# Expert stage of a two-block transformer kernel: every piece of the down weights split in full, the low part of the features on GpSimd

## The reference

```python
def hier_moe(h, wg, bg, we, be, w_gate, w_up, w_down):
    ...
    ids = (g_sel * EXPERTS_PER_GROUP + top_i).reshape(-1).astype(jnp.int32)
    order = jnp.argsort(ids)
    tok = order // TOP_K
    xs = xf[tok]
    hg = lax.ragged_dot(xs, w_gate.astype(xs.dtype), sizes)
    hu = lax.ragged_dot(xs, w_up.astype(xs.dtype), sizes)
    ys = lax.ragged_dot(jax.nn.silu(hg) * hu, w_down.astype(xs.dtype), sizes)
    ys = ys * gates.reshape(-1)[order][:, None].astype(ys.dtype)
    y = jax.ops.segment_sum(ys, tok, num_segments=t)
```

## Time and profile before

| | |
|---|---|
| median of 3 runs | 1083.66 us (1079.57 to 1084.92) |
| the profiled execution | 1080.93 us, its span 1079.1 us |
| PE (matmul) busy | 1034.6 us, 96% of the span |
| DVE busy | 842.9 us, 78% |
| ACT busy | 665.2 us, 62% |
| POOL busy | 33.0 us, 3% |
| first and last transposes of the hidden values in a full unit | start 622.28 and 1035.19 us |

### The profile page before, as it was taken

How to read it: one execution, slowest core, us unless ns; L and a number is a source line. 1 busy time by engine, 2 the same in 40 slices (tenths; PEclk the granted TensorE clock), 3 DMA queues, 4 the chain that set the end, 5 groups by cost and what they waited for, 6 DMA issues and landing times. The chain is left out here.

```text
span 1079.1 us, 14950 instructions
## 1 busy us (share of the span) xinstructions
PE 1034.6 (96%) x5574; PEld 872.7 (81%) x5574; DVE 842.9 (78%) x1091; ACT 665.2 (62%) x832; POOL 33.0 (3%) x40
## 2 busy tenths in 40 slices
PE   7999999999998899989889999999999999999996
PEld 6777999999998777889778787878787777878775
DVE  5855766766777556677757889999999899999977
ACT  5554655555555645556333677777777777777764
POOL 1001000000000100100020000000000000000000
PEclk9999999999999999999999999999999999999999
DMA  9634545646424443233311789989998998999881
GB/s 349 244 117 137 194 169 184 196 157 234 156 91 150 158 144 130 81 118 118 117 32 34 285 327 368 371 348 390 349 388 351 374 363 352 378 359 386 339 318 43
DMA packets 82711, 253.61 MB, mean 235 GB/s; under 512 B 4160, under 2 KB 42176, under 8 KB 62656
## 3 DMA queue, kind: packets, MB, share of 16 engines
q1 hardware_dynamic: 82624, 252.50, 62.2%
HBM read 251.44 MB, written 1.05 MB: 234 GB/s over the span
## 5 line engine op out<-in xcount | busy, mean ns | idle before, releaser
L1021 DVE TENSOR_TENSOR WL<-raw,WH 128x2048 fp32r<-128x2048 f32 x232 | 497.5, 2175 | 110.0 <-ACT WH L543 109.7
L543 ACT ACTIVATE WH<-raw 128x2048 fp32r<-128x2048 f32 x232 | 421.5, 1823 | 91.2 <-PE bank L1910 74.9
L1908 PE MATMUL bank<-WH,MXH 128*128 128x512 f32 x552 | 219.4, 397 | 1.6 <-DVE CV L1316 0.9
L1910 PE MATMUL bank<-WH,MXL 128*128 128x512 f32 x552 | 216.0, 391 | 0.0
L1909 PE MATMUL bank<-WL,MXH 128*128 128x512 f32 x552 | 215.5, 390 | 0.0
L1908 PE MATMUL bank<-HTH,WH 128*128 128x256 f32 x576 | 166.1, 288 | 6.2 <-DVE CV L1316 2.6
L1910 PE MATMUL bank<-HTH,WL 128*128 128x256 f32 x576 | 163.6, 284 | 0.0
L1909 PE MATMUL bank<-HTL,WH 128*128 128x256 f32 x576 | 163.6, 284 | 0.0
L1908 PE MATMUL bank<-WH,HTH 128*128 128x512 f32 x348 | 139.7, 401 | 7.2 <-DVE HTL L1044 2.4
L1909 PE MATMUL bank<-WL,HTH 128*128 128x512 f32 x348 | 137.1, 394 | 0.0
L1908 PEld LDWEIGHTS bank<-WH,MXH 128*128 128x128 f32 x552 | 104.4, 189 | 23.2 <-issue 2.3
(11 more groups left out here) (393 smaller groups left out, 1098.6 us busy)
## 6 DMA issues: line engine op xcount, KB each, us to landing
raw<-in_exp_w_up SPq DMA_DIRECT2D x52, 1024.0 KB, 7.6
raw<-in_exp_w_gate SPq DMA_DIRECT2D x52, 1024.0 KB, 8.1
raw<-in_exp_w_down SPq DMA_DIRECT2D x52, 1024.0 KB, 6.7
raw<-in_w_in SPq DMA_DIRECT2D x34, 1024.0 KB, 5.1
raw<-in_w_up SPq DMA_DIRECT2D x22, 1024.0 KB, 5.4
raw<-in_w_down SPq DMA_DIRECT2D x11, 1024.0 KB, 5.2
raw<-in_w_out SPq DMA_DIRECT2D x8, 1024.0 KB, 5.0
raw<-in_w_o SPq DMA_DIRECT2D x4, 1024.0 KB, 5.6
```

What stands on the lines that cost most here:

```text
L543: e.activation(WH[i % HL][:, 0:n], raw[i % RAW][:, 0:n], ACT.Copy).then_inc(a_wh, 1)
L1021: e.tensor_tensor(l, r, h.bitcast(F32), ALU.subtract).then_inc(v_wl, 1)
L1908: e.matmul(out_, ah, bh, start=start, stop=False)
L1910: return e.matmul(out_, al, bh, start=False, stop=stop)
```

## The change

Of the down weights every piece is split in full, and the hidden values with them (512 columns instead of 384), so the native products and the plain copy in `TMP` are gone; `is_mixed` goes, and SP's loads wait for the low part alone. GpSimd gets a unit loop of its own and makes the features' low part for the units from 2 on (two tensor_tensors of 128x512 from `XST` and the high part, each after its own copy on ScalarE). On ScalarE the copy of d1 moves from the end of a unit to the next unit (or the last one), behind that unit's features and norm column.

```diff
-def is_mixed(i):
-
-    return i >= unit_base(1) and (i - unit_base(1)) % 6 == 5
...
-        hidden = HTH[:, 0:6, :].rearrange("p a b -> p (a b)").rearrange("p (i k c) -> p i k c", i=4, k=3)
+        hidden = HTH[:, :, :].rearrange("p a b -> p (a b)").rearrange("p (i k c) -> p i k c", i=4, k=4)
...
+        def features_low(u, tile, k):
+
+            xs4, ks = XST[k].rearrange("p k (t c) -> p k t c", t=NT), slice(4 * k, 4 * k + 4)
+            return (XCL[u % 2][:, ks, :].unsqueeze(2), xs4[:, :, bass.ds(tile, 1), :],
+                    XCH[u % 2][:, ks, :].bitcast(F32).unsqueeze(2))
...
-                    e.wait_ge(*((p_used, j + 1) if is_mixed(j) or is_native(j) else (v_wl, split_count(j))))
+                    e.wait_ge(*((p_used, j + 1) if is_native(j) else (v_wl, split_count(j))))
...
-                n = PC // 2 if is_mixed(i) else PC
-                e.activation(WH[i % HL][:, 0:n], raw[i % RAW][:, 0:n], ACT.Copy).then_inc(a_wh, 1)
+                e.activation(WH[i % HL][:, :], raw[i % RAW][:, :], ACT.Copy).then_inc(a_wh, 1)
...
-                e.activation(HIH[u % 2], bank[TBK][:, 0:384].rearrange("p (k c) -> p k c", k=3),
-                             ACT.Copy)
-                e.activation(TMP[:, u % 2, 0:128], bank[TBK][:, 384:512], ACT.Copy).then_inc(a_tmpc, 1)
+                e.activation(HIH[u % 2], bank[TBK][:, :].rearrange("p (k c) -> p k c", k=4),
+                             ACT.Copy).then_inc(a_hih, 1)
 
             def unit(u):
...
                 if u > 1:
+                    split(i - 1)
                     split(i)
                     split(i + 1)
...
                 split(i + 4)
-                split(i + 5)
 
             def last_unit(u):
                 i = unit_base(u + 1)
+                split(i - 1)
                 split(i)
                 turn_hidden(u)
...
-                n = PC // 2 if is_mixed(i) else PC
-                r, h, l = raw[i % RAW][:, 0:n], WH[i % HL][:, 0:n], WL[i % HL][:, 0:n]
-                e.tensor_tensor(l, r, h.bitcast(F32), ALU.subtract).then_inc(v_wl, 1)
+                e.tensor_tensor(WL[i % HL][:, :], raw[i % RAW][:, :], WH[i % HL][:, :].bitcast(F32),
+                                ALU.subtract).then_inc(v_wl, 1)
...
-                e.wait_ge(a_tmpc, u + 1)
+                e.wait_ge(a_hih, u + 1)
                 if u > 1:
                     e.wait_ge(p_used, unit_base(u))
-                e.tensor_tensor(HIL[u % 2], bank[TBK][:, 0:384].rearrange("p (k c) -> p k c", k=3),
+                e.tensor_tensor(HIL[u % 2], bank[TBK][:, :].rearrange("p (k c) -> p k c", k=4),
                                 HIH[u % 2].bitcast(F32), ALU.subtract).then_inc(v_hil, 1)
...
                 if u > 1:
                     load_tile(u)
                     load_code(u)
-                    features_low(u)
                     e.wait_ge(v_hid, u - 1)
...
+            def unit(u):
+                tile = e.value_load(TBI[u:u + 1, 1:2], min_val=0, max_val=NT - 1)
+                if u == 2:
+                    e.wait_ge(s_xcl, 2)
+                for k in range(2):
+                    e.wait_ge(a_xch, 2 * u + 1 + k)
+                    m = e.tensor_tensor(*features_low(u, tile, k), ALU.subtract)
+                m.then_inc(s_xcl, 1)
+
+            def more(u):
+                with e.If(count > u):
+                    unit(u)
+                    if u + 1 < UNITS:
+                        more(u + 1)
+
+            for u in range(2, LEAST):
+                unit(u)
+            more(LEAST)
             row_powers("out")
...
-                for k in range(3):
+                for k in range(4):
...
                         m = three(bank[banks[hf]][:, :], HIH[u % 2][:, k, :], HIL[u % 2][:, k, :], wh[:, k % 2, hs],
-                                  wl[:, k % 2, hs], k == 0, False)
-                    if k == 1:
+                                  wl[:, k % 2, hs], k == 0, k == 3)
+                    if k % 2:
                         m.then_inc(p_used, 1)
-                w = raw[(i + 1) % RAW][:, PC // 2:PC]
-                for hf in range(2):
-                    m = e.matmul(bank[banks[hf]][:, :], TMP[:, u % 2, 0:128], w[:, hf * 512:(hf + 1) * 512], start=False,
-                                 stop=True)
-                m.then_inc(p_used, 1)
```

More of the change, by code:

```diff
@@ L429, in build @@
                                                      "sege", "vv", "og", "gsq", "emx", "stc", "ogt", "nexp", "csq", "cum"))
-        a_xth, a_route, a_xst, a_selT, a_xch, a_sg, a_tmpc, a_yh, a_selL, a_fo = (
-            sem("a_" + n) for n in ("xth", "route", "xst", "selT", "xch", "sg", "tmpc", "yh", "selL", "fo"))
+        a_xth, a_route, a_xst, a_selT, a_xch, a_sg, a_hih, a_yh, a_selL, a_fo = (
+            sem("a_" + n) for n in ("xth", "route", "xst", "selT", "xch", "sg", "hih", "yh", "selL", "fo"))
         v_wl, v_ms, v_h0, v_coll, v_ang, v_ropm, v_rope, v_lam, v_nm, v_sm, v_pml, v_ors, v_on, \
@@ L439, in build @@
                                                   "gz", "gn", "cum", "mn", "sv", "gh", "xa"))
-        v_xtl, v_route, v_sel, v_xst, v_gm, v_xc, v_gs, v_hid, v_hil, v_yg, v_yl, v_xg, v_fo = (
-            sem("v_" + n) for n in ("xtl", "route", "sel", "xst", "gm", "xc", "gs", "hid", "hil", "yg", "yl", "xg", "fo"))
+        v_xtl, v_route, v_sel, v_xst, v_gm, v_gs, v_hid, v_hil, v_yg, v_yl, v_xg, v_fo = (
+            sem("v_" + n) for n in ("xtl", "route", "sel", "xst", "gm", "gs", "hid", "hil", "yg", "yl", "xg", "fo"))
         g_rstd, g_xsd, g_vm, g_vc, g_wr, g_yz = (sem("g_" + n) for n in ("rstd", "xsd", "vm", "vc", "wr", "yz"))
+        s_xcl = sem("s_xcl")
         own_v, own_a = (sem("own_" + n) for n in "va")
@@ L1690, in vector @@
                                     XC0[0][:, 4 * k:4 * k + 4, :].bitcast(F32), ALU.subtract)
-            m.then_inc(v_xc, 1)
+            m.then_inc(s_xcl, 1)
             gathered(3)
@@ L1730, in gate_hidden @@
                                        op0=ALU.mult, op1=ALU.mult).then_inc(v_hid, 1)
[L1732 to L1740, removed]
             load_tile(1)
-            features_low(1)
+            e.wait_ge(a_xch, 4)
+            for k in range(2):
+                m = e.tensor_tensor(*features_low(1, tile[1], k), ALU.subtract)
+            m.then_inc(s_xcl, 1)
             og, ig = (bc(v.unsqueeze(1), P, NT, 32) for v in (off, inc))
@@ L1903, in gpsimd @@
             row_powers("n2")
+            e.wait_ge(v_route, V_ROUTE["units"])
+            count = e.value_load(TBI[0:1, 3:4], min_val=0, max_val=UNITS)
+            def unit(u):
+                tile = e.value_load(TBI[u:u + 1, 1:2], min_val=0, max_val=NT - 1)
+                if u == 2:
+                    e.wait_ge(s_xcl, 2)
+                for k in range(2):
+                    e.wait_ge(a_xch, 2 * u + 1 + k)
+                    m = e.tensor_tensor(*features_low(u, tile, k), ALU.subtract)
+                m.then_inc(s_xcl, 1)
+            def more(u):
[6 more added lines that the diff above has]
+            more(LEAST)
             row_powers("out")
@@ L2431, in unit @@
                 if u:
-                    e.wait_ge(v_xc, u + 1)
+                    e.wait_ge(s_xcl, u + 1)
                 for b in range(2):
@@ L2451, in unit @@
                         e.wait_ge(a_xst, 10)
-                        e.wait_ge(v_xc, 1)
+                        e.wait_ge(s_xcl, 1)
                     for kh in range(2):
```

## The result

Changed kernel: median 1089.09 us (9 runs); the kernel before on the same chips 1080.60 us (9 runs). Ratio 1.0077, 95% interval 1.0056 to 1.0097: slower by 0.8%, 8.5 us. The forecast was plus 6.9 us, on top of a median of three runs (1083.66) that nine runs put at 1080.60.

The account below looks back on a forecast made before the run. TensorE was taken to set the pace at 17.20 us a unit, VectorE having little in hand. Units plus 3.4 (period 17.34) and the end plus 3.5 gave plus 6.9 on 1083.66: 1090.6 us, range 1078 to 1113.

Parts of the forecast that it names:

- TensorE, minus 0.36: Expert stage, TensorE: 1.72 us of native products go, six split products (1.36) come, minus 0.36 a unit.
- The run on VectorE and the two-unit cycle: VectorE's unbroken run from d1's to u0's remainder delays TensorE every second unit: 17.34 a unit with the collision, plus 3.4 us.
- GpSimd's first part loses VectorE 0.26: Expert stage: GpSimd's first feature part runs 10.92 to 11.96; VectorE wants d1's remainder at 11.70, losing at least 0.26.
- The second part costs nothing: Expert stage: GpSimd's second feature part runs 14.16 to 15.20 beside VectorE's gating, for nothing.
- Gating to g0's remainder 1.09: VectorE, after d1's remainder: gating, two register loads, gate column and their gap take 1.09 together, to 14.99.
- The end, plus 3.5: Last unit: d1's copy stands behind the branch; TensorE's last piece plus 3.9, less 0.36 for native products: plus 3.5 us once.
- Loads: Weight loads from HBM: 363 GB/s asked at 17.34 us, nothing on the path, nothing gained.
- VectorE never binds: Expert stage: VectorE's run ends before 22.8 instead of 23.48; 24 x -0.36 = -8.6, 1078.6 us in all; chance 0.16.
- Both parts in front: GpSimd keeps its turn for both parts, d1's remainder waits 1.30: 18.23 a unit, plus 28.2, 1111.9 us; chance 0.22.
- The change moves the load, not the bound: ScalarE's late d1 copy keeps u0's wait even with GpSimd silent: 17.21 a unit, 1087.4 us in all; chance 0.14.

Follow-up runs that it names:

- run 2: Changed kernel without the features' low part from unit 2 on, and with d1's copy at its unit's end again: 1073.22 us, ratio 0.9914.
- run 1: Changed kernel without the features' low part from unit 2 on (GpSimd does nothing in the stage): 1079.94 us, ratio 0.9978.
- run 3: Changed kernel, GpSimd's low parts kept, with ScalarE copying d1 before the features again, as before the change: 1100.37 us, ratio 1.0179.
- run 8: Changed kernel, d1's copy at its unit's end, features copied one unit ahead, low parts half on GpSimd, half in VectorE's gap: 1073.43 us, ratio 0.9922.
- run 6: Changed kernel with d1's copy before the features and VectorE adding the down results behind u0's remainder: 1084.04 us, ratio 1.0020.
- run 5: Kernel before, native products kept, with only the features' low parts moved to a unit loop on GpSimd: 1082.46 us, ratio 1.0015.
- run 4: Changed kernel with the features' low parts back on VectorE, behind the register loads, and no GpSimd loop: 1098.93 us (one run).

## Why the prediction was right, step by step

The direction and the mechanism were right; that the sum came so close was luck. The units cost 6.1 us where I had 3.4, the end 1.1 where I had 3.5: two errors of 2.7 and 2.4 that cancel. Inside the first term errors cancel again.

**TensorE, minus 0.36:** right. Run 2 measured 0.349. The period without waits is 16.855; I had 16.84.

**The run on VectorE and the two-unit cycle:** right in kind and place. The forecast was a wait at u0's remainder with periods alternating about 17.34; the trace has a wait in front of u0 in each unit (0.45 and 0.24 above) and periods of 17.34 and 17.57 in turn. ScalarE's order gave the places I had worked out: the copy of d1 9.68 after the unit's start (9.74), VectorE's d1 at 11.61 (11.70). From the end of g1 to the start of u0 in the next unit I had 17.84 with the collision; the trace has 17.98 (TensorE ends g1 5.94 after 745.85, at 751.79; 769.77 - 751.79). The failed terms were within it:

- *GpSimd's first part loses VectorE 0.26:* it lost 0.37. It held VectorE for 1.10, not 1.04, and VectorE was ready a little sooner.
- *The second part costs nothing, since it runs beside the gating and the register loads:* it cost 0.37 of g0's remainder.
- *Gating to g0's remainder 1.09:* it was 0.72 (760.76 - 760.04). The loads stood in the open before the change only because the remainder in front of the gating was a half one. Now they run beside a full one. The chain of waits of the changed kernel shows them (DVEq is VectorE's sequencer):

```profile
758.26 0.30 DVEq L1718
758.60 0.19 DVEq L1718
758.88 0.32 DVEq L1721
759.23 0.19 DVEq L1721
```

  Lines 1718 and 1721 are the two loads, 758.26 to 759.4, inside the remainder of 757.46 to 760.12. The last two errors are the same 0.37, once each way. By the times the second is there because of the first: without the loads' gap g0's remainder comes 0.37 sooner and meets GpSimd, which is done at 761.13, just when that remainder would have come with the gap. No run tried this by itself.
- *Left out:* TensorE starts u0 0.15 after the end of its remainder in every unit (769.62 to 769.77), where I had 0.04. And after a wait its first product takes about 0.1 longer before the next can start: 0.31 at u0, 0.34 for the step 1058.64 to 1058.98 below, instead of 0.23. In the cycle of two units that comes once: 34.92 is 17.98 and 16.94, and run 2's unit is 16.855.

Together the cycle is 34.92 (17.34 + 17.57, rounded) instead of 34.68, and the term 6.1 us instead of 3.4. By the cycle: collisions 0.75 instead of 0.26 (plus 0.49), the loads' gap minus 0.37, VectorE ready sooner minus 0.09, TensorE's start plus 0.11 and its slow product plus 0.1, together 0.24. So the collision was mis-sized by almost a factor of three, and the rest of VectorE's run was too long by about half of that: without GpSimd I had 17.21, run 1 measured 17.083.

**The end, plus 3.5:** mis-sized; it is plus 1.08. The order of events was right (ScalarE's branch now stands in front of d1's copy, TensorE waits for d1), the price of VectorE's branch was not. Timelines of ScalarE, VectorE and TensorE at the end of the units, changed kernel:

```profile
1049.47 1.91 ACT L545 ACTIVATE WH<-raw 128x2048 fp32r<-128x2048 f32 x1
1054.35 3.71 ACT L545 ACTIVATE WH<-raw 128x2048 fp32r<-128x2048 f32 x2 [2.96 <-issue]
...
1056.30 2.29 DVE L1021 TENSOR_TENSOR WL<-raw,WH 128x2048 fp32r<-128x2048 f32 x1 [2.58 <-ACT WH L545]
1058.51 0.75 DVE L1730 SCALAR_TENSOR_TENSOR CV<-bank,sm,CV 128x512 f32<-128x512 f32 x1
1059.35 2.29 DVE L1021 TENSOR_TENSOR WL<-raw,WH 128x2048 fp32r<-128x2048 f32 x1
1063.57 0.69 DVE L1771 TENSOR_TENSOR HTH<-bank,HTH 128x512 fp32r<-128x512 f32 x1 [1.93 <-ACT HTH L953]
...
1058.64 0.50 PE L1922 MATMUL bank<-WH,HTH 128*128 128x512 f32 x1 [1.11 <-DVE WL L1021]
1058.98 0.39 PE L1923 MATMUL bank<-WL,HTH 128*128 128x512 f32 x1
...
1067.72 0.50 PE L1922 MATMUL bank<-WH,HTH 128*128 128x512 f32 x1 [0.39 <-DVE WL L1021]
```

ScalarE needs 4.88 from copy to copy (I took 5.25), VectorE only 0.84 from the gating to the next remainder, where the earlier trace rows have 4.95. So TensorE's last piece starts 1067.72 - 1042.74 = 24.98 after the last full unit's start against 23.53 (1058.55 - 1035.02): +1.45, less the 0.36 of the native products. I had carried a gap over as if it were the price of the branch.

VectorE's sequencer takes the branch while the engine still works: in the changed kernel at 1056.43, early in d1's full remainder, in the kernel before at 1046.63, late in the half one. From there to the next instruction it was 2.91 and 5.36 us, of which 2.07 and 0.42 lay beside the remainder. VectorE's branch isn't even on the path any more: VectorE waits 1.93 for the hidden values' copy on ScalarE (1063.57), and that waits for the transposes behind d1 on TensorE.

By the chain of waits the end now pays for ScalarE's branch, behind which d1's copy starts at 1054.35. Runs 1 and 2 have the place of d1's copy as their only difference, and there the end is 45.60 against 42.52, plus 3.1. Against the kernel before it is less, partly because VectorE's restart there came 0.93 after ScalarE's copy had ended (1052.00 and 1051.07 in the earlier trace rows); in run 2 it comes 0.03 after. The rest between these ends wasn't taken apart.

**Loads:** right, nothing. At a period of 16.855 us run 2 moves 373 GB/s. That also settles the rule that I had set aside: the Trainium skill's page SBUF — State Buffer gives HBM to one core as about 358 GB/s (the section on the bandwidth-pool intuition), and the windows rows shown here are above it in every kernel: 365 before, 361 after, 373 in run 2.

**The rivals:** *VectorE never binds* didn't happen, but run 2 shows its time: 16.855. *Both parts in front* (18.23) didn't: VectorE's d1 asked before the second part and got its turn. Run 3 shows the other case, in which the second part asked first. *The change moves the load, not the bound* is a piece of the truth: 0.228 of the 0.604 that were given back is ScalarE's order alone.

The sum came to 6.9 against a measured difference of 8.5 in the medians; of the profiled pair, 7.2 are the change's and 1.6 are scatter ahead of it. The forecast of the whole is better than either of its terms.

## What to carry to other kernels

Before counting on shorter work of the bound engine, work out its supplier's longest unbroken run and what it feeds, not its busy share: the change moved a copy later, put two collisions in that run, and so cost 0.60 us a unit where it saved 0.35. Work for GpSimd goes beside VectorE's instructions that have an operand in a PSUM bank (run 8), and a supplier's other work goes behind the piece that is waited for (run 6); run 8, with half of the low part on GpSimd and half in a gap of VectorE, turned +0.8% into -0.8%. A gap read in one trace (a branch, a register load) isn't the price of the instruction: it is what was not covered there.

## What was not expected of the hardware

- Between a VectorE instruction on two SBUF operands and GpSimd, the one that asks first goes first, also between two VectorE instructions that are back to back (5.94 for a pair of 4.48, and 2.32 for a half of 1.22). A tensor_tensor of 128x512 on GpSimd held VectorE for 1.08 to 1.10 us where it could be read (the result's unit, runs 3 and 5), though its record was up to 3.3 us long: GpSimd's records hold the waiting.
- A gap at the branch out of the units has no fixed length. VectorE's, from the gating to the next remainder, was 4.95 us before, 5.17 in run 5, 1.57 in run 4, 0.84 in the changed kernel and 0.82 in run 1. From its branch to the next instruction it was 5.36, 5.59, 3.00, 2.91 and 2.89: two values, of which more or less lay beside the instructions in front. In the other runs (2.59 in run 2, 2.50 in run 3) VectorE waited for ScalarE's copy, so its branch can't be read there. ScalarE's gap, from the start of the copy in front to the start of the next, was 4.2 to 5.7 us where it showed, but in run 4 no more than 2.9. Why it is long in some kernels and short in others wasn't tried and stays open.
